# Hybrid retention and latent-attention block: the order of the eight query blocks of an attention head

## The reference

```
def attend(args):
    q_blk, b = args                                   # one block of 128 queries
    q_chunk = (b * Q_BLOCK + jnp.arange(Q_BLOCK)) // CHUNK
    mask = key_chunk[None, :] <= q_chunk[:, None]     # causal by chunks of 64
    s = jnp.einsum('bqhd,bkhd->bhqk', q_blk, k) * scale
    s = jnp.where(mask[None, None], s, neg)
    prob = jax.nn.softmax(s, axis=-1)
    return jnp.einsum('bhqk,bkhe->bqhe', prob, v)
out = lax.map(attend, (qb, jnp.arange(nb)))           # nb = 8 blocks
```

## Time and profile before

| what | us |
|---|---|
| median of 3 runs | 1350.97 (1349.43 to 1351.02) |
| the profiled execution's own time | 1351.96 |
| its span, first to last instruction | 1350.2 |
| PE busy | 1284.6 (95% of the span) |
| DVE busy | 665.4 (49%) |
| ACT busy | 438.6 (32%) |
| POOL busy | 301.5 (22%) |

### The profile page before, as it was taken

The page is one execution under the profiler, slowest core; times in us unless marked ns, Lnnn a source line. Parts: engine busy times, 40 slices in busy tenths (PEclk is TensorE's granted clock), DMA queues, the critical chain, the costliest instruction groups (busy, mean ns, idle before and its releaser), DMA issues.

```text
span 1350.2 us, 17263 instructions
## 1 busy us (share of the span) xinstructions
PE 1284.6 (95%) x6172; PEld 1080.0 (80%) x6172; DVE 665.4 (49%) x1188; ACT 438.6 (32%) x817; POOL 301.5 (22%) x425
## 2 busy tenths in 40 slices
PE   5999999988998999999999999999899999988996
PEld 4888878877888888878888888888688888877885
DVE  4644434466656326753334343333376667765123
ACT  4621222135656214533333333333302112133122
POOL 1334434431000002442222232221000000141122
PEclk9999989989999999999999999999899999989999
DMA  7211110010011400232233222331322222430002
GB/s 269 76 32 48 32 46 31 0 39 1 0 62 63 141 0 1 78 94 71 71 94 94 87 62 86 94 94 65 123 94 98 104 96 94 140 125 16 0 32 93
DMA packets 88020, 96.12 MB, mean 71 GB/s; under 512 B 3856, under 2 KB 68240, under 8 KB 87952
## 3 DMA queue, kind: packets, MB, share of 16 engines
q1 hardware_dynamic: 87808, 94.95, 22.0%
q10 hardware_dynamic: 144, 0.26, 0.1%
HBM read 79.47 MB, written 15.73 MB: 71 GB/s over the span
## 4 chain that ended last, share of the span: by engine, by line
PE 77%; issue 11%; POOL 7%; DVE 3%; ACT 1%; DMA 1%; POOLq 0%; SPq 0%; ACTq 0%; DVEq 0%
PE PS L1489 10%; PE PS L1490 10%; PE PS L1491 10%; PE PS L1651 6%; PE PS L1653 6%; PE PS L1652 6%; PE PS L194 3%; PE PS L859 3%; PE PS L196 3%; PE PS L195 3%; PE PS L875 2%; PE PS L1898 2%; PE PS L1899 2%; PE PS L1897 2%; POOL X L544 2%
## 5 line engine op out<-in xcount | busy, mean ns | idle before, releaser
L1237 DVE TENSOR_TENSOR X<-X,PS 128x512 f32<-128x512 f32 x192 | 131.4, 686 | 127.3 <-PE PS L1653 74.7
L194 PE MATMUL PS<-WF,HTH 128*128 128x512 f32 (+1 forms) x448 | 178.0, 397 | 2.2 <-ACT X L319 1.5
L196 PE MATMUL PS<-WF,HTL 128*128 128x512 f32 (+1 forms) x448 | 174.4, 389 | 0.0
L195 PE MATMUL PS<-WF,HTH 128*128 128x512 f32 (+1 forms) x448 | 174.1, 389 | 0.0
L1489 PE MATMUL PS<-HTH,WF 128*128 128x512 f32 x336 | 130.7, 389 | 0.0
L1490 PE MATMUL PS<-HTL,WF 128*128 128x512 f32 x336 | 130.7, 389 | 0.0
L1491 PE MATMUL PS<-HTH,WF 128*128 128x512 f32 x336 | 130.7, 389 | 0.0
L1489 PE MATMUL PS<-WF 128*128 128x512 f32 x252 | 98.1, 389 | 2.6 <-issue 2.6
L194 PEld LDWEIGHTS PS<-WF,HTH 128*128 128x128 f32 x448 | 85.2, 190 | 17.7 <-issue 1.9
L1491 PE MATMUL PS<-WF 128*128 128x512 f32 x252 | 98.1, 389 | 0.0
L1490 PE MATMUL PS<-WF 128*128 128x512 f32 x252 | 98.1, 389 | 0.0
(11 more groups left out here) (223 smaller groups left out, 2678.6 us busy)
## 6 DMA issues: line engine op xcount, KB each, us to landing
RAW<-in_w_ffn_gate SPq DMA_DIRECT2D x22, 512.0 KB, 4.2
RAW<-in_w_ffn_up SPq DMA_DIRECT2D x22, 512.0 KB, 5.4
hid<-TMP SPq DMA_DIRECT2D x44, 256.0 KB, 2.1
RAW<-hid SPq DMA_DIRECT2D x22, 512.0 KB, 3.2
RAW<-in_w_ffn_down SPq DMA_DIRECT2D x22, 512.0 KB, 3.5
X<-in_x SPq DMA_DIRECT2D x16, 512.0 KB, 4.9
RAW<-in_w_in SPq DMA_DIRECT2D x32, 256.0 KB, 3.1
RAW<-in_w_o SPq DMA_DIRECT2D x16, 256.0 KB, 3.3
```

The lines of the kernel that those rows point to most:

```text
L194: nc.tensor.matmul(dst, HTH[:, k, tok], w_h, start=(k == 0), stop=False)
L195: nc.tensor.matmul(dst, HTH[:, k, tok], w_l, start=False, stop=False)
L196: last = nc.tensor.matmul(dst, HTL[:, k, tok], w_h, start=False, stop=(k == K - 1))
L1237: nc.vector.tensor_tensor(x, x, src, ALU.add).then_inc(done, 1)
```

## The change

The blocks of each of the four heads are taken in the order 0, 7, 1, 6, 2, 5, 3, 4. The counter of the loops, now i, is the place in this order. What depends on the place (banks, the halves of TMP and PT, the statistics' columns, all semaphore counts) goes by i; what depends on the block (its queries, how many keys it sees, where its output goes) goes by TORD[i]. The programs of the engines otherwise keep their order.

```
+        TORD = (0, 7, 1, 6, 2, 5, 3, 4)
...
         def pe_head(e, h, early, after):
-            def scores(t):
-                if t == 0:
+            def scores(i):
+                t = TORD[i]
+                if i == 0:
                     e.wait_ge(a_lo, h * 4 + 4)
-                if t in (0, 2):
-                    e.wait_ge(a_qr, h * 2 + (2 if t else 1))
-                if t >= 2:
-                    e.wait_ge(a_exp, h * T + t - 1)
+                if i < 2:
+                    e.wait_ge(a_qr, h * 2 + 1 + i)
+                if i >= 2:
+                    e.wait_ge(a_exp, h * T + i - 1)
...
+            def turn(i):
+                e.wait_ge(a_prob, h * T + i + 1)
+                e.wait_ge(a_pt, h * T + i)
+                for j in range(TORD[i] + 1):
...
+            def values(i):
+                t = TORD[i]
+                e.wait_ge(a_vh, h * 2 + (1 if t < 2 else 2))
+                e.wait_ge(a_pt, h * T + i + 1)
+                e.wait_ge(a_o_lo, h * T + max(0, i - 1))
...
             scores(0)
             scores(1)
-            for t in range(T):
-                if t + 2 < T:
-                    scores(t + 2)
+            for i in range(T):
+                if i + 2 < T:
+                    scores(i + 2)
...
         def dve_head(e, h, early, after):
-            def biggest(t):
-                e.wait_ge(a_scores, h * T + t + 1)
-                e.wait_ge(a_exp, h * T + max(0, t - 1))
-                src = score_banks(t)
-                nb, n = seen(t)
+            def biggest(i):
+                e.wait_ge(a_scores, h * T + i + 1)
+                e.wait_ge(a_exp, h * T + max(0, i - 1))
+                src = score_banks(i)
+                nb, n = seen(TORD[i])
...
             biggest(0)
             biggest(1)
             divide(0)
```

More of the change, by code:

```diff
@@ L835, in seen, with score_banks @@
             return (1, (t + 1) * P) if t < 4 else (2, (t + 1) * P // 2)
-        def score_banks(t):
-            nb, n = seen(t)
-            b = 2 * ((t + 1) % 2)
+        TORD = (0, 7, 1, 6, 2, 5, 3, 4)
+        def score_banks(i):
+            nb, n = seen(TORD[i])
+            b = 2 * ((i + 1) % 2)
             return PS[:, b:b + nb, 0:n]
         def pe_head(e, h, early, after):
-            def scores(t):
-                if t == 0:
+            def scores(i):
+                t = TORD[i]
+                if i == 0:
                     e.wait_ge(a_lo, h * 4 + 4)
-                if t in (0, 2):
-                    e.wait_ge(a_qr, h * 2 + (2 if t else 1))
-                if t >= 2:
-                    e.wait_ge(a_exp, h * T + t - 1)
+                if i < 2:
+                    e.wait_ge(a_qr, h * 2 + 1 + i)
+                if i >= 2:
+                    e.wait_ge(a_exp, h * T + i - 1)
                 tok = slice(t * P, t * P + P)
@@ L855, in scores @@
                     blk = slice(c * n, c * n + max(n, 2 * P))
-                    dst = bank(2 * ((t + 1) % 2) + c, max(n, 2 * P))
-                    for i, (a, b) in enumerate(((QT[0], KT[0]), (QT[0], KT[1]), (QT[1], KT[0]),
+                    dst = bank(2 * ((i + 1) % 2) + c, max(n, 2 * P))
+                    for m, (a, b) in enumerate(((QT[0], KT[0]), (QT[0], KT[1]), (QT[1], KT[0]),
                                                 (QR, CT[0][:, 3]), (QR, CT[1][:, 3]))):
-                        last = nc.tensor.matmul(dst, a[:, tok], b[:, blk], start=(i == 0), stop=(i == 4))
+                        last = nc.tensor.matmul(dst, a[:, tok], b[:, blk], start=(m == 0), stop=(m == 4))
                 last.then_inc(a_scores, 1)
-            def turn(t):
-                e.wait_ge(a_prob, h * T + t + 1)
-                e.wait_ge(a_pt, h * T + t)
-                for j in range(t + 1):
[L866 to L875, removed]
+            def turn(i):
+                e.wait_ge(a_prob, h * T + i + 1)
+                e.wait_ge(a_pt, h * T + i)
+                for j in range(TORD[i] + 1):
+                    last = nc.tensor.transpose(PS[:, 4 + j // 4, (j % 4) * P:(j % 4) * P + P],
+                                               tmp((i % 2) * 1024 + j * P, P), ident)
+                last.then_inc(a_turn, 1)
+            def values(i):
[3 more added lines that the diff above has]
+                e.wait_ge(a_o_lo, h * T + max(0, i - 1))
+                for j in range(t + 1):
+                    last = nc.tensor.matmul(bank(6 + i % 2, P), VH[:, j], PT[i % 2][:, j * P:j * P + P], start=(j == 0), stop=(j == t))
                 last.then_inc(a_pv, 1)
@@ L879, in pe_head @@
             scores(1)
-            for t in range(T):
-                if t + 2 < T:
-                    scores(t + 2)
+            for i in range(T):
+                if i + 2 < T:
+                    scores(i + 2)
                 else:
                     e.wait_ge(a_exp, h * T + T - 1)
[L886 to L889, removed]
+                    early(i + 2 - T)
+                if i >= 1:
+                    values(i - 1)
+                turn(i)
             e.wait_ge(a_exp, h * T + T)
@@ L894, in act_head @@
         def act_head(e, h, early, late, after):
[L895 to L901, removed]
@@ L903, in out_hi, with exp @@
-            def out_hi(t):
-                e.wait_ge(a_pv, h * T + t + 1)
+            def exp(i):
+                e.wait_ge(a_bias, h * T + i + 1)
+                e.wait_ge(a_turn, h * T + max(0, i - 1))
+                nb, n = seen(TORD[i])
+                dst = tmp((i % 2) * 1024, nb * n).rearrange("p (b n) -> p b n", b=nb)
+                nc.scalar.activation(dst, score_banks(i), ACT.Exp, bias=ST[:, 76 + i % 2:77 + i % 2],
+                                     scale=SCALE, accum_out=ST[:, 78 + i % 2:79 + i % 2]).then_inc(a_exp, 1)
@@ L905, in out_hi @@
+            def out_hi(i):
+                t = TORD[i]
+                e.wait_ge(a_pv, h * T + i + 1)
                 nc.scalar.copy(HTH[:, bass.ds(h + 4, 1), t * P:t * P + P],
-                               bank(6 + t % 2, P).unsqueeze(1)).then_inc(a_o_hi, 1)
+                               bank(6 + i % 2, P).unsqueeze(1)).then_inc(a_o_hi, 1)
             exp(0)
[L909 to L914, removed]
+            for i in range(T):
+                if i + 1 < T:
+                    exp(i + 1)
+                if i >= 1:
+                    out_hi(i - 1)
+                if i == 3:
@@ L915, in act_head @@
                     early()
-                if t == T - 1:
+                if i == T - 1:
                     late()
-                e.wait_ge(a_turn, h * T + t + 1)
-                e.wait_ge(a_pv, h * T + max(0, t - 1))
-                n = (t + 1) * P
+                e.wait_ge(a_turn, h * T + i + 1)
+                e.wait_ge(a_pv, h * T + max(0, i - 1))
+                n = (TORD[i] + 1) * P
                 src = PS[:, 4:6, :].rearrange("p b n -> p (b n)")[:, 0:n]
-                nc.scalar.copy(PT[t % 2][:, 0:n], src).then_inc(a_pt, 1)
+                nc.scalar.copy(PT[i % 2][:, 0:n], src).then_inc(a_pt, 1)
@@ L926, in dve_head @@
         def dve_head(e, h, early, after):
-            def biggest(t):
-                e.wait_ge(a_scores, h * T + t + 1)
-                e.wait_ge(a_exp, h * T + max(0, t - 1))
-                src = score_banks(t)
-                nb, n = seen(t)
+            def biggest(i):
+                e.wait_ge(a_scores, h * T + i + 1)
+                e.wait_ge(a_exp, h * T + max(0, i - 1))
+                src = score_banks(i)
+                nb, n = seen(TORD[i])
                 nc.vector.memset(src[0:CHUNK, nb - 1, n - CHUNK:n], MASKED).then_inc(a_mask, 1)
-                e.wait_ge(a_mask, h * T + t + 1)
-                nc.vector.tensor_reduce(ST[:, 74 + t % 2:75 + t % 2], src, mybir.AxisListType.XY if nb > 1 else AXX,
+                e.wait_ge(a_mask, h * T + i + 1)
+                nc.vector.tensor_reduce(ST[:, 74 + i % 2:75 + i % 2], src, mybir.AxisListType.XY if nb > 1 else AXX,
@@ L936, in biggest, with out_lo @@
                                         ALU.max).then_inc(a_max, 1)
-                e.wait_ge(a_max, h * T + t + 1)
-                nc.vector.tensor_scalar(ST[:, 76 + t % 2:77 + t % 2], ST[:, 74 + t % 2:75 + t % 2], -SCALE, None,
+                e.wait_ge(a_max, h * T + i + 1)
+                nc.vector.tensor_scalar(ST[:, 76 + i % 2:77 + i % 2], ST[:, 74 + i % 2:75 + i % 2], -SCALE, None,
                                         ALU.mult).then_inc(a_bias, 1)
[L941 to L944, removed]
+            def out_lo(i):
+                e.wait_ge(a_o_hi, h * T + i + 1)
+                d = slice(TORD[i] * P, TORD[i] * P + P)
+                nc.vector.tensor_tensor(HTL[:, bass.ds(h + 4, 1), d], bank(6 + i % 2, P).unsqueeze(1),
@@ L945, in out_lo, with divide @@
                                         HTH[:, bass.ds(h + 4, 1), d].bitcast(F32), ALU.subtract).then_inc(a_o_lo, 1)
[L947 to L953, removed]
+            def divide(i):
+                e.wait_ge(a_exp, h * T + i + 1)
```

(13 more changed lines are left out.)

## The result

| | before | after |
|---|---|---|
| median, us | 1350.99 (4 runs, 1349.43 to 1352.23) | 1361.05 (4 runs, 1359.64 to 1364.23) |
| profiled execution, us | 1351.96 | 1360.86 |
| its span | 1350.2 | 1359.0 |
| stage 3b, first scores to first matmul of stage 4 | 120.28 | 129.34 |

A forecast was written before the change was run, and what follows sets the result against it. PE was taken as the bound, so its idle time inside heads counts. Three heads at 2.25 us plus 1.35 gave 8.1, or 9.5 with a larger start; 8.8 was taken: 1360.8 profiled, 1359.8 median, range 1356 to 1365 us.

The forecast's parts named there:

- Start of a head: Before block 6's scores PE waits for block 7's exponential, idling 2.35 us instead of 1.1: +1.25 us a head.
- Copy of turn 7: Block 7's values wait for ACT's copy of turn 7, covered only by block 2's scores: +0.4 us a head.
- End of a head: Shorter last values cover less of the wait for DVE's split before the next head's first scores: +0.6 us.
- Head 3: Last head: +1.25 and +0.4 at its start; at its end waits shorten by 0.6 and one grows 0.3: +1.35 us.
- The clock, no new fall: PE's new idle stretch of 2.4 us in every head causes no new fall of the granted clock: zero us.
- The sum: Heads 0 to 2 cost 6.75 us and head 3 1.35: 8.1, or 9.5 with a larger start term; 8.8 taken.
- The rival of the clock: The clock falls in heads 1 to 3, 3.3 to 4.5 us more, about 1364 us; chance 0.17.
- Faster: Block 7's scores cover the first softmax chain, removing the 1.1 us wait at each head's third scores: 1346 us; chance 0.03.
- no difference: In the heads, PE's new waits replace the old ones one for one, leaving the time unchanged; chance 0.04.

The follow-up runs named there:

- filled kernel: Changed kernel plus 16 unread identity transposes in each head's gap on PE; 1359.50 us, ratio 1.0067 to the kernel before, and 1359.45 us when run again.
- joined kernels: The kernel before with heads joined across the seam, 1346.12 us; that with head 3 turning four retention tiles at places 6 and 7, 1344.36 us.

## Why the prediction was right

- *Start of a head, +1.25.* Right. Block 6's scores start 6.07 us into the head (388.77 - 382.70) where I had 6.04; the wait is in the two pieces forecast around one transpose. Halving the maximum, dividing first and moving block 7 alone each agree that one chain sets it, that of block 7, and that neither the division nor alternation does.
- *Copy of turn 7, +0.4.* Right: 1.39 us from the scores of block 2 to the values of block 7, of which 1.0 is work.
- *End of a head, +0.6.* Right: 3.87 us for my 3.85, with 2.5 of work by my count. The short block last, by itself, cost 0.5 a head.
- *Head 3, +1.35.* The mechanism was right: at full clock it takes 33.47 us (filled kernel), +1.30. It took 35.09, since the clock fell.
- *The clock, no new fall.* This step failed for head 3. I had weighed one idle stretch of 2.55 us without a fall against head 0's fall and gone with the former. The fall came, and recurred, in head 3 of both profiles of the changed kernel. Its price there, 1.6 us (35.09 - 33.47), was just over my 1.1 to 1.5. At the same time head 0's old fall was gone, -1.1, the lower end that I had named for it. I took zero for both; they sum to +0.5. The row that I had leaned on was also one profile's chance: at the same place PE stood idle for 2.98 us in the changed kernel's profile and for 2.22 in its second, and both times the clock fell (rows in the last section). That fall stands in stages 4 to 6, which I had called unchanged in length and which took 1.3 us more.
- *The sum.* 8.1 us of terms, 0.5 of clock and 0.15 in each of heads 0 to 2 (some 0.1 of it at the values of block 6, the rest I cannot name) make 9.05, and stage 3b measures 9.06. I forecast 8.8 by adding half of the spread of the start's term. The start's term needed no such reserve; it was used up by the clock and the unnamed 0.15. That 8.8 came within 0.3 us is in part luck; the waits of 2.25 a head are not. The medians say 10.1, within the scatter of some 2 us between runs of one kernel.
- *The rival of the clock* (falls in heads 1 to 3, 1364) was a third right: one head of three. With the gap in one piece, as in the kernel that divides first, it was right in three of four heads. The Trainium skill (TensorE: Matmul & The Clock Gate, section HAM oscillation — how this bites in real kernels) describes a kernel in which the wait between bursts, of 3 to 5 us, puts the clock down at each; the runs here, with shorter waits, agree in part: it recurs, but only in some heads, and in the changed kernel in one of four.
- *Faster* and *no difference*: the wait at the third scores did go, and another twice as long took its place one step later, as the rival's own condition said.

## What to carry to other kernels

Order blocks of unequal size by what stands behind each on the engine that sets the pace: a large block needs work queued between its own matmuls and the next step that needs its result, so it may come late or last, not second. At the end the long block earns its place, as its final product covers the hand-over to the next unit. If a loop's units each pay a start and an end, join them across the seam before reordering inside: here that gave 4.5 us, and reordering the last head's end as well brought it to 6.3, where none of the four other orders tried beat the ascending one.

## What the runs showed of the hardware

TensorE's granted clock fell to 1.2 GHz after an idle gap of 2.0 to 2.2 us in some heads, where the same gap in other heads of the same kernel did nothing. The changed kernel's head 3, its gap (most of it in the first window) and what follows (windows of 2 us, columns as in rows 2; 0.50 is 1.2 GHz):

```profile
418.00:420.00 2.00, 0.33 (x1) 0.14 (x1) 1.86 (x7) 1.09 (x2) 0.00 (x0) 1.00 1.03 420
420.00:422.00 2.00, 1.84 (x7) 1.70 (x8) 0.94 (x3) 0.73 (x5) 0.00 (x0) 0.78 0.73 283
422.00:424.00 2.00, 2.00 (x8) 1.83 (x8) 0.41 (x2) 0.06 (x1) 0.00 (x0) 0.50 0.04 12
424.00:426.00 2.00, 2.00 (x13) 1.70 (x11) 1.57 (x5) 1.02 (x2) 0.00 (x0) 0.87 0.00 0
```

It recurs: two profiles of each kernel had the falls in the same heads (3; and 0, 1 and 3 with an undivided gap of 2.23 us). The undivided gap brought more falls than the one with a transpose in its middle (one head of four; also one, head 2, with block 7 alone moved; none where the first piece was 0.97). Transposes that nobody reads, in place of standing still, kept 1.00 in all heads of three profiles and lengthened nothing, 1.6 us a fall saved.

A gap of that length isn't needed. Head 0 of the kernel before fell after idle times of 1.51 and 0.66 us with the first two scores, 1.4 us, between them; so did head 0 of the kernel with block 4 last and of the one that alternates late. The two joined kernels have 1.43 and 0.66 there: the one with the end of head 3 changed fell, the other didn't.

What decides in which head it falls wasn't found. The idle times alone don't, by the two joined kernels, whose stage 3b began at 320.00 and 318.48 us. Nor does the moment alone: head 0 of the changed kernel and of the one that alternates late both begin at 319.85, and only the latter's falls. That the falls came back in the same heads may owe to the moment too, since in each pair of profiles stage 3b began within 0.5 us of the same time.

The idle stretch of 2.55 us in the kernel before (rows 9), after which the clock stayed at 1.00, shows how little one profile says. In the changed kernel's profile it is 2.98 us long, up to 585.37, and the clock falls behind it (0.50 from 586 to 588; the row is of 10 us):

```profile
580.00:590.00 10.00, 7.02 (x25) 5.42 (x24) 9.73 (x8) 3.56 (x7) 9.03 (x7) 0.83 0.07 27
```

Of the fourteen profiles of this document eight have a fall at this place, after 2.2 to 3.6 us of idle time, and six have none, after 1.8 to 2.7.
